# GpSimd's modulation products and sums in another order, with seven drains a piece, and the column sums loaded behind the out weights

## What is computed

```python
def adaln(cond, mod_w, mod_b):
    m = jax.nn.silu(cond) @ mod_w + mod_b
    return jnp.split(m, 6, axis=-1)
...
sh1, sc1, g1, sh2, sc2, g2 = [m[:, None, :] for m in adaln(c, mod_w[i], mod_b[i])]
a = modulate(h_lat, norm1_g[i], sh1, sc1)
```

## Time and profile before

| what | us |
|---|---|
| median of 3 runs | 1934.0 (1932.85 to 1935.17) |
| the profiled execution | 1937.97 |
| its span | 1935.9 |
| TensorE busy | 1893.6 (98% of the span) |
| GpSimd busy | 792.2 (41%) |
| GpSimd products L397, 448 of them | 272.6 |
| GpSimd sums L401, 336 of them | 248.0 |
| GpSimd last sums L403, 56 of them | 42.0 |
| TensorE's mean granted clock | 0.992 |

### The profile page before, as it was taken

How to read it: one execution, slowest core, us unless ns; L and a number is a source line. 1 busy time by engine, 2 the same in 40 slices (tenths; PEclk the granted TensorE clock), 3 DMA queues, 4 the chain that set the end, 5 groups by cost and what they waited for, 6 DMA issues and landing times.

```text
span 1935.9 us, 26176 instructions
## 1 busy us (share of the span) xinstructions
PE 1893.6 (98%) x9836; PEld 1013.4 (52%) x9836; DVE 770.1 (40%) x1646; ACT 543.5 (28%) x1187; POOL 792.2 (41%) x1091
## 2 busy tenths in 40 slices
PE   9999999999999999999999999999999999999998
PEld 6545556566546555565655456664543444445433
DVE  1544443433220454343446463633453311234524
ACT  3134433122422234431225231651211122012110
POOL 1767677775756667676710012760111100001111
PEclk9989999999999999999999999999899999998999
DMA  7322333334335243333422422313699832055997
GB/s 294 118 102 104 138 136 109 112 139 150 139 127 175 106 173 127 129 138 110 168 91 101 160 82 87 121 62 157 258 370 373 320 120 87 0 217 195 381 367 313
DMA packets 70299, 322.16 MB, mean 166 GB/s; under 512 B 8680, under 2 KB 11174, under 8 KB 55590
## 3 DMA queue, kind: packets, MB, share of 16 engines
q1 hardware_dynamic: 41688, 216.22, 29.8%
q0 software_dynamic: 25328, 92.81, 13.9%
q10 hardware_dynamic: 3168, 11.54, 1.5%
HBM read 287.51 MB, written 33.03 MB: 166 GB/s over the span
## 4 chain that ended last, share of the span: by engine, by line
PE 90%; DVE 4%; DMA 3%; ACT 1%; issue 1%; POOL 1%; DVEq 0%; POOLq 0%; SPq 0%; ACTq 0%
PE psA L462 24%; PE psA L1861 10%; PE psA L454 9%; PE psA L2008 7%; PE psA L1902 6%; PE psA L627 6%; PE psSO L2027 4%; PE psT L441 3%; PE psA L503 3%; PE psSO L532 3%; PE psSO L542 2%; PE psT L1977 1%; PE psSO L2208 1%; PE psSO L565 1%; PE psSO L600 1%; PE psSO L2233 1%
## 5 line engine op out<-in xcount | busy, mean ns | idle before, releaser
L462 PE MATMUL psA<-gB,pool_mem 128*128 128x512 f32 x1024 | 456.1, 598 | 0.0
L397 POOL TENSOR_TENSOR pool_mem<-pool_mem,cs 128x256 f32<-128x256 f32 x448 | 272.6, 641 | 132.6 <-DMA pool_mem<-in_mod_w 132.1
L462 PEld LDWEIGHTS psA<-gB,pool_mem 128*128 128x128 f32 x1024 | 189.8, 190 | 224.7 <-issue 224.7
L401 POOL TENSOR_TENSOR pool_mem<-pool_mem 128x256 f32<-128x256 f32 x336 | 248.0, 765 | 33.7 <-issue 25.7
L1861 PE MATMUL psA<-pool_mem 128*128 128x512 f32 (+1 forms) x528 | 209.0, 554 | 1.9 <-DVE pool_mem L1617 1.1
L454 PE MATMUL psA<-pool_mem,gB 128*128 128x256 f32 (+2 forms) x768 | 189.7, 403 | 2.2 <-ACT gB L796 1.2
L1810 POOL DMA_INDIRECT pool_mem<-xs_scratch,idx x38 | 35.7, 939 | 333.3 <-DVE idx L2632 304.9
L454 PEld LDWEIGHTS psA<-pool_mem,gB 128*128 128x128 f32 x768 | 143.8, 190 | 44.6 <-issue 6.6
L1861 PEld LDWEIGHTS psA<-pool_mem 128*128 128x128 f32 x528 | 99.2, 190 | 105.1 <-issue 99.8
L2008 PE MATMUL psA<-pool_mem 128*32 128x512 f32 (+1 forms) x896 | 141.1, 593 | 0.0
L1902 PE MATMUL psA<-pool_mem 128*128 128x512 f32 x256 | 113.9, 595 | 0.8 <-issue 0.8
(11 more groups left out here) (359 smaller groups left out, 2466.6 us busy)
## 6 DMA issues: line engine op xcount, KB each, us to landing
pool_mem<-in_w_gu SPq DMA_DIRECT2D x32, 2048.0 KB, 12.3
pool_mem<-in_mod_w POOLq DMA_DIRECT2D x56, 1024.0 KB, 7.8
pool_mem<-in_w_dn SPq DMA_DIRECT2D x32, 1024.0 KB, 14.0
pool_mem<-in_w_qk SPq DMA_DIRECT2D x24, 1024.0 KB, 4.9
ys_scratch<-pool_mem ACTq DMA_DIRECT2D x22, 512.0 KB, 10.2
pool_mem<-in_odd_w_in SPq DMA_DIRECT2D x5, 2048.0 KB, 9.7
pool_mem<-in_w_out SPq DMA_DIRECT2D x4, 2048.0 KB, 8.0
macc_scratch<-pool_mem POOLq DMA_DIRECT2D x56, 128.0 KB, 2.0
```

The source lines that it names most:

```text
L397: nc.gpsimd.tensor_tensor(wm[:, b, k], wm[:, b, k], c_all[:, k].to_broadcast([P, MCH]), ALU.mult)
L401: nc.gpsimd.tensor_tensor(wm[:, b, k], wm[:, b, k], wm[:, b, n + k], ALU.add)
L462: m = nc.tensor.matmul(psA[:, n % 2, :], w(i), src[:, k, :], start=(i == 0), stop=(i == len(ks) - 1))
```

## The change

In `multiply` the fifteen operations stay, in another order. Products k and 4 + k stand together; from k = 1 on, the addition of the preceding pair follows them; each such group ends in a drain. Then come the fourth addition and the first of the 2 + 2 with a drain, the second of the 2 + 2 with a drain, and the last addition with its drain. So a piece has seven drains where it had four. In SyncE's queue of layer 1 the wait for all stores and the first two loads of the column sums move behind the first half of the out weights.

```diff
@@ sync @@
                     load(0, d["w_v"][L, hp + 1], KD * 256)
+                sp.wait_ge(pa_ready, base + pa_qk(3, 1, 1) + 1)
+                load(OUT_SLOT[0], d["w_out"][L, 0], KD * 512)
                 if L + 1 == DEPTH:
                     sp.wait_ge(m_stored, 16 * (MACC // MCH))
                     sums_in(0)
                     sums_in(1)
-                sp.wait_ge(pa_ready, base + pa_qk(3, 1, 1) + 1)
-                load(OUT_SLOT[0], d["w_out"][L, 0], KD * 512)
                 sp.wait_ge(pa_ready, base + pa_v(3, 3) + 1)
                 load(0, d["w_gb"][L, 3], KD * P)
@@ gpsimd, multiply @@
-                for k in range(KD):
+                def times(k):
                     nc.gpsimd.tensor_tensor(wm[:, b, k], wm[:, b, k], c_all[:, k].to_broadcast([P, MCH]), ALU.mult)
+
+                def plus(k, n):
+                    nc.gpsimd.tensor_tensor(wm[:, b, k], wm[:, b, k], wm[:, b, n + k], ALU.add)
+
+                for k in range(4):
+                    times(k)
+                    times(4 + k)
+                    if k:
+                        plus(k - 1, 4)
+                    pool.drain()
+                plus(3, 4)
+                plus(0, 2)
                 pool.drain()
-                for n in (4, 2):
-                    for k in range(n):
-                        nc.gpsimd.tensor_tensor(wm[:, b, k], wm[:, b, k], wm[:, b, n + k], ALU.add)
-                    pool.drain()
+                plus(1, 2)
+                pool.drain()
                 nc.gpsimd.tensor_tensor(macc[:, b], wm[:, b, 0], wm[:, b, 1], ALU.add)
                 pool.drain()
```

## The result

The changed kernel takes 2004.8 us (median of 6 runs, 1992.7 to 2010.3), the kernel before, run beside it, 1934.6 us (6 runs, 1932.9 to 1942.4). The ratio is 1.033 (95%: 1.030 to 1.035; the quotient of the two medians is 1.036): slower by 3.3%, where 1926.6 and "faster" had been forecast. Here and in the experiments, two executions far above all others of their kernels (7022 us in e3, and 2458 us of the kernel before beside e9 and e10) are left out of the ratios.

What follows compares the result with a forecast made beforehand. TensorE was taken to bound the kernel, only its waits and lower clock paying: gains of 3.5 + 2.3 + 1.6 = 7.4 us, from the median 1934.0, gave 1926.6 us; 8-in-10 range 1921 to 1938.

Steps and rivals of the forecast that it cites:

- What bounds the kernel: TensorE, busy 98% of the span: only its standing still or lower clock matters; the length of GpSimd's modulation bounds nothing.
- The cover: Ahead of VectorE's fold of the identity: 41 us of added GpSimd time, 0.73 us a piece, before TensorE loses time.
- The loads: SyncE's queue: out weights still go at 993.6 whatever the modulation does; the swap by itself gains and costs nothing.
- The holds: VectorE operations at b=1 run starts: held 1.2 us, not 4.6; TensorE's waits before L676 and L542 shrink, gaining 7.4 us.
- rival (b): Every VectorE operation stays clear of a run's start; both TensorE waits and clock losses go: 12.2 us, 1921.8; chance 0.15.
- rival (a): VectorE's hold is not cut, or unprofiled runs have no such holds: time stays at 1934.0; chance 0.25.
- The price of the drains: GpSimd's pieces: three new drains behind additions, 0.19 us each, 31 us over 56 pieces; taken as +31 to +35, ends +20, +60.
- Rival (c): Modulation too late for the fold: three new drains at 0.38 us each, 64 us more over 56 pieces: 1950; chance 0.13.

Runs made afterwards that it cites:

- e3: Changed kernel with seven drains a piece, but the first behind six products instead of two: 1941.7 us, ratio 1.004 to the kernel before.
- e9: Interleaved order without drains, semaphores instead, both stores behind the second half, SyncE's order as in the change: 1930.5 us, ratio 0.994 to the kernel before.
- e10: Kernel before with both stores behind the second half, the same kernel as e4 on another chip: 1931.7 us, ratio 0.995.
- e7: Kernel before with GpSimd's new order alone, SyncE's queue as before: 1995.7 us, ratio 1.033.
- e2: Changed kernel, but both loads of a pair must land before its first half begins: 2024.4 us, ratio 1.048 to the kernel before.
- e8: Kernel before with one drain added right behind the first half's store: 1950.3 us, ratio 1.008.
- e5: Changed kernel, first drain of each piece replaced by a wait for the second product's semaphore: 1936.0 us, ratio 1.001 to the kernel before.
- e6: Kernel before with the new order and seven drains in the second halves only, first halves in the old order: 1931.0 us, ratio 1.000.
- e1: Kernel before with SyncE's new order alone, out weights ahead of the column sums: 1933.7 us, ratio 1.001.
- e4: Kernel before with both stores of a pair behind the second half, products and drains as before: 1926.3 us, ratio 0.997.

## Why the prediction was wrong

**What bounds the kernel** held: TensorE's waits, not GpSimd's length, decide, until GpSimd is later than the cover.

**The cover** held, too. It was put at 41 us of added GpSimd time. Added time (last store less 978.3) less the measured wait of TensorE gives it for each late kernel. With the 11.7 us by which VectorE was early in the changed kernel, where the forecast put 7.4, its formula gives 36.7, and 37.5 was measured:

| kernel | last store | added | TensorE's wait | cover |
|---|---|---|---|---|
| changed | 1079.4 | 101.1 | 63.6 | 37.5 |
| e7 | 1086.2 | 107.9 | 68.2 | 39.7 |
| e2 | 1113.6 | 135.3 | 96.5 | 38.8 |
| e8 | 1036.1 | 57.8 | 21.9 | 35.9 |
| e5 | 1023.3 | 45.0 | 6.1 | 38.9 |
| e3 | 1028.3 | 50.0 | 6.3 | 43.7 |
| e6 | 1013.0 | 34.7 | none | over 34.7 |

**The loads**: right. The swap is worth nothing (e1), and in e7 even the case that it guards against costs nothing.

**The holds**: they were cut as forecast, but the gain in time isn't shown. Forecast were a wait of 2.2 us before L676 (measured 1.84), no wait before L542 (none), and 3.0 us of clock kept as lost: these came back. A wait of 1.84 us here, of 2.22 in e9 and of 2.27 in e6 (at 94.9) had the granted clock of 1.00 behind it, while a wait of 2.13 in e6's second layer (at 646.3) had 0.50 for 3.4 us. So the neighbour that I took, a wait of 2.18 elsewhere, was no measure for this place. 7.4 us was the forecast, 11.7 came between the two profiled executions, near the 12.2 of the whole-gain rival (b). But that nearness is partly luck: e1 was 8.3 us early at the fold without any change of GpSimd's order. And in the medians of e6, with cut holds and no wait at the fold, nothing came (1.000, 0.997 to 1.002). That is what rival (a) says of executions whose phases make no costly hold. So the runs don't show that the change would have been faster had its drains cost what I put; of the kernels that are in time for the fold, only those without any hold (e4, e10, e9) gained, 0.3 to 0.6%.

**The price of the drains** is the step that failed. Of its two terms one held: behind an addition a drain makes the step 0.87 us, and the product-to-addition step was 0.57, the lower of my ends. The other, that "the new piece has as before one drain behind products alone, whose step stays", was wrong. What it costs depends on how long behind the DMA issues it stands, because it waits for their landing: 74 us in all, against nothing in the sum. So GpSimd's +20 to +60 became +101, some 60 us past the cover. I had the rule that a drain holds the queue until what was issued before it is done, and read "what was issued" as the fifteen operations; the DMAs that the same engine had issued belong to it. The first drain's idle time in the trace of before (0.34 us typical, but 2.22 at 149.62) was read at one piece alone; the 7 of 56 pieces in which the landing came last pointed at it.

**Rival (c)** foresaw the shape, VectorE at the fold and TensorE behind it, and had 0.13. Its cause, that all three new drains are dearer (0.38 each), was wrong, and its 1950 with it. The range was too narrow because both ends of the modulation's length came from the prices of drains next to arithmetic.

The rule weighed against the change, the one-instruction lock of the Trainium skill's page "SBUF — State Buffer", section "Who interferes with whom", is not borne out by the lengths: holds of 1.9, 4.2 and 5.2 us go with runs of two, six and eight GpSimd instructions. Where nothing is held for a run, as in e4, the lengths do fit it: 1.0 us an addition, some tenths more than free. Timelines of VectorE and GpSimd in the changed kernel, the longest that is left:

```profile
358.53 1.93 DVE L1016 TENSOR_TENSOR pool_mem<-pool_mem 128x512 f32<-128x512 f32 x1
...
358.09 0.60 POOL L424 DMA_DIRECT2D macc_scratch<-pool_mem  x1 [0.81 <-issue]
358.71 1.19 POOL L398 TENSOR_TENSOR pool_mem<-pool_mem,cs 128x256 f32<-128x256 f32 x2
```

VectorE's addition begins during the store's descriptor work and ends at 360.46, 0.56 us behind the run of two that follows it; free it takes 0.69 us. All operations of over 1.6 us in the traces with a store ahead of the run began like this, between 0.39 us ahead of the run's start and 0.05 behind it. Not every operation there is held: in e1 a L1003 that began at 463.65, at the end of a store's descriptor work, took its usual 0.69 us.

## What to carry to other kernels

Before a drain is moved forward in an engine's stream, list the DMAs which that engine has issued and which are still under way there: a drain that stood behind enough work to hide their landing becomes a wait for them. Where only one operation's result is wanted, a semaphore on that operation waits for nothing else. And look at the spread of a cost over all its instances, not at one: the seven drains of the kernel before that ended with a landing held the answer.

## What the runs showed of the hardware

- A drain of GpSimd waits for the landing of the DMAs that GpSimd itself issued: 56 of 56 first drains in either trace fit it. Where the landing came last they ended 0.18 us behind a load's or 0.08 behind a store's. One with only the store's descriptor work ahead of it (0.69 us) took 2.23 us, the store landing after 2.1 (e8).
- A VectorE operation that stands between GpSimd's descriptor work for a store and products directly behind it can be held for the whole run of products: four operations in the trace of before, three in e1, one in e3. A drain (changed kernel) or a semaphore wait (e5) behind two products ended the hold there. Without a store directly ahead (e4, e10), or with a drain between (e8), none of the 28 runs of eight in each trace held anything; nor did e9's other order, with no store ahead. Why some operations there go free, and why the pair is not given back between instructions stays open: no run here took the store away and kept the descriptor work, or the reverse.
- A semaphore wait between two products cost 0.12 us over the plain step of 0.57 (e5). The first drain of a piece cost 0.46 in e2, where both loads had landed; a drain behind an addition, later in a piece, 0.19.
